# Smaller units for the last input weights, a first expert gathered already transposed, and two residual products moved into the last expert steps

## The reference

```
h = RMSNorm(x)
q,k,v,xr,yr,gates = split(h @ w_in + b_in)
A = attention(rope(rms(q)), rope(rms(k)), v)            # 8 heads, 2 kv heads
R = (rglru_fwd(conv(xr)) + rglru_bwd(conv(xr))) * gelu(yr)
merged = sig(g_A) * (A @ w_attn_o) + sig(g_R) * (R @ w_lru_o)
x = x + merged @ w_out
x = x + MoE(RMSNorm(x))     # top 4 of 32 experts, each w_gu 1024x2048, w_down 1024x1024
out = RMSNorm(x)
```

## Time and profile before

| | |
|---|---|
| runs of the kernel | 1135.7, 1138.17, 1138.58 us; median 1138.17 |
| span of the profiled execution | 1134.2 us (its own device time is not listed; the three runs read 1.5 to 4.4 us more than this span) |
| PE busy | 96% of the span |
| bytes from HBM | 438.2 MB |
| mean granted clock of TensorE | 0.986 |

### The profile page before, as it was taken

One profiled execution on the slowest core, in us unless ns is written; L12 is line 12 of the kernel. 1 busy time (PEld: TensorE's weight loads), 2 busy tenths in 40 slices (PEclk: granted clock), 3 DMA queues, 4 the chain that ended last, 5 costly groups with the idle time before them and its releaser, 6 DMA issues.

```text
span 1134.2 us, 12887 instructions
## 1 busy us (share of the span) xinstructions
PE 1084.8 (96%) x5407; PEld 503.4 (44%) x5407; DVE 371.1 (33%) x645; ACT 237.2 (21%) x369; POOL 2.6 (0%) x10
## 2 busy tenths in 40 slices
PE   7999999999999999999998989898989899899987
PEld 7999899633333333333333333333333333333332
DVE  6997887522212222122121211111211212121212
ACT  5399961211111111111111110011110101010102
POOL 0000000000000000000000000000000000000000
PEclk9999999899999999999999999999999999999999
DMA  9544277999999999999999999999999999999996
GB/s 353 185 178 149 84 287 300 419 425 399 431 425 428 426 434 432 433 426 435 431 429 436 430 430 436 429 430 436 430 432 433 429 436 430 427 427 429 426 428 247
DMA packets 25637, 439.77 MB, mean 388 GB/s; under 512 B 3425, under 2 KB 4065, under 8 KB 6273
## 3 DMA queue, kind: packets, MB, share of 16 engines
q1 hardware_dynamic: 24976, 438.27, 91.5%
q10 hardware_dynamic: 624, 0.99, 0.2%
HBM read 438.20 MB, written 1.05 MB: 387 GB/s over the span
## 4 chain that ended last, share of the span: by engine, by line
PE 67%; DMA 28%; DVE 2%; SPq 1%; ACT 1%; issue 0%; DVEq 0%
PE ps L1491 26%; DMA slots<-in_w_down_dram 22%; PE ps L1500 13%; PE ps L1172 13%; DMA slots<-in_w_gu_dram 5%; PE ps L1455 5%; PE ps L1436 3%; PE ps L1549 2%; DVE slots_r L725 1%; SPq L403 1%; PE ps L1229 1%; PE ps L1450 1%; PE ps L1414 1%; PE ps L1234 0%; PE ps L1526 0%; PE ps L1274 0%
## 5 line engine op out<-in xcount | busy, mean ns | idle before, releaser
L1500 PE MATMUL ps<-slots,lru 128*64 128x512 f32 x1024 | 239.8, 610 | 17.2 <-DMA slots<-in_w_down_dram 17.2
L1491 PE MATMUL ps<-slots,lru 128*64 128x512 f32 x1024 | 227.7, 594 | 11.7 <-DMA slots<-in_w_gu_dram 11.2
L1491 PE MATMUL ps<-slots,qT 128*64 128x512 f32 x984 | 223.8, 596 | 4.6 <-DMA slots<-in_w_gu_dram 4.6
L1491 PEld LDWEIGHTS ps<-slots,lru 128*64 128x64 f32 x1024 | 74.1, 137 | 160.8 <-issue 139.7
L1491 PEld LDWEIGHTS ps<-slots,qT 128*64 128x64 f32 x984 | 68.9, 137 | 152.2 <-issue 144.8
L1500 PEld LDWEIGHTS ps<-slots,lru 128*64 128x64 f32 x1024 | 68.5, 139 | 142.5 <-issue 123.5
L1100 DVE COPY lru<-ps 128x512 f32<-128x512 f32 x32 | 22.1, 692 | 322.9 <-PE ps L1491 322.9
L1172 PE MATMUL ps<-slots_r 128*128 128x256 f32 (+1 forms) x812 | 107.7, 291 | 0.2 <-DVE slots_r L725 0.2
L1172 PEld LDWEIGHTS ps<-slots_r 128*128 128x128 f32 x812 | 102.2, 191 | 5.4 <-issue 2.5
L653 ACT ACTIVATE lru<-ps 128x512 f32<-128x512 f32 x32 | 19.1, 598 | 395.3 <-PE ps L1491 395.3
L1082 DVE TENSOR_SCALAR lru<-sq,rank_col,small 128x64 f32<-128x64 f32 x64 | 17.2, 312 | 241.8 <-PE ps L1436 241.8
(11 more groups left out here) (200 smaller groups left out, 649.3 us busy)
## 6 DMA issues: line engine op xcount, KB each, us to landing
slots<-in_w_gu_dram SPq DMA_DIRECT2D x40, 4096.0 KB, 29.2
slots<-in_w_gu_dram SPq DMA_DIRECT2D x44, 2048.0 KB, 18.9
slots<-in_w_down_dram SPq DMA_DIRECT2D x20, 4096.0 KB, 28.4
slots<-in_w_down_dram SPq DMA_DIRECT2D x22, 2048.0 KB, 20.8
slots<-in_pre_dram SPq DMA_DIRECT2D x13, 2048.0 KB, 8.2
slots<-in_w_down_dram SPq DMA_DIRECT2D x8, 512.0 KB, 31.0
slots<-in_pre_dram SPq DMA_DIRECT2D x3, 1024.0 KB, 6.9
slots<-in_w_gu_dram SPq DMA_DIRECT2D x3, 1024.0 KB, 17.4
```

The costliest lines, as they stand in the source:

```text
L1491: ins = nc.tensor.matmul(ps[64 * side:64 * side + 64, 4 + b, :], xgT[i % 2][:, k, :], rows[r][:, o:o + BANK], start=(k == 0), stop=(k == K ...
L1500: ins = nc.tensor.matmul(ps[64 * side:64 * side + 64, bank, :], actT[(i - 1) % 2][:, k, :], w[:, r, side * BANK:(side + 1) * BANK], start= ...
```

## The change

1. **Units.** Chunks 0 to 7 stay as they are. The seven later chunks become 14 units of 1 MB. A unit needs one slot alone: it lands in the slot's first half, its high part goes to the slot's second half. Each has its own condition for the load (`UNIT_FREED`) and its own two splits. The first four units (projection columns) are read in pieces of 1 KB for a partition and row.
2. **Expert loads.** Slots 2 and 3 are no longer used by input weights once `group` 23 is done, so expert chunks 0 and 1 are issued there; `late` and half of `pbuf` are loaded once the recurrent branch and attention are done; the other slots follow one at a time with the `mix` steps. SLOT_ORDER changes with it.
3. **Mix.** `mix(0)` no longer stands between `branches(3)` and `branches(4)`; six `mix` steps are followed by `mix_end` over the last two blocks.
4. **First expert.** `first_gather` multiplies each 128x128 block of `x2` (as the stationary operand) with the selection (64 columns), which gives the gathered tokens already transposed; ACT's copy, four transposes and one wait go.
5. **Residual products.** The four products before and in step 0 go. In the last four steps, step i = 0 does banks 0 and 1 and step i = 2 does banks 2 and 3, between `gate_up` 2 and `gate_up` 3. The first scatter opens the banks in their place.

```diff
-        SLOT_ORDER = [2, 3, LOWS, SLOTS - 1, 0, 1, 4, 5]
+        UNIT_SLOT = [4, 5, 0, 1, 4, 5, 0, 1, LOWS, 4, 5, 0, 1, LOWS]
+        UNIT_FREED = [(group_done, 16), (group_done, 16), (group_done, 20), (group_done, 20), (group_done, 26),
+                      (group_done, 28), (group_done, 30), (group_done, 32), (gate_ps, 32), (branch_ps, 2),
+                      (branch_ps, 3), (branch_ps, 4), (branch_ps, 6), (branch_ps, 7)]
+        SLOT_ORDER = [2, 3, 4, 5, 0, 1, LOWS, SLOTS - 1]
+        FREED = {2: (group_done, 24), 4: (branch_ps, KD), 5: (mixed_ps, 1), 0: (mixed_ps, 2), 1: (mixed_ps, 3),
+                 LOWS: (mixed_ps, 4)}
...
+            for u in range(4):
+                unit_load(u)
+            for k in range(2):
+                expert_load(k)
+            for u in range(4, 7):
+                unit_load(u)
+            sp.wait_ge(rec_ok, 2)
+            sp.wait_ge(pv_ps, NQ // 2)
             n, j = step_of(EXTRA[0])
             sp.dma_start(late[:, :], expert_src(n, j)).then_inc(extra_full[0], 16)
+            half_load(extra_rows(1, 0), EXTRA[1], 0, extra_full[1])
+            unit_load(7)
+            unit_load(8)
+            half_load(wide[:, 0:2048], 7, 0, slot_full[SLOTS - 1])
+            for u in range(9, 14):
+                unit_load(u)
...
+            def unit_split_high(u):
+                act.wait_ge(*unit_landed(u))
+                nc.scalar.activation(unit_high(u), unit_whole(u), ACT.Copy).then_inc(split_hi, 1)
...
-            gathered_copy(0)
...
-                if g == 1:
-                    split_low(12)
-                if g == 3:
-                    split_low(13)
-                if g == KD - 1:
-                    split_low_by_halves(14)
+                if g != 3:
+                    unit_split_low(7 + g if g < 3 else 6 + g)
...
-            for g in range(4):
+            for g in range(KD):
                 branches(g)
-            mix(0)
-            for g in range(4, KD):
-                branches(g)
-            for c in range(1, 4):
+            for c in range(ENDS):
                 mix(c)
...
+            def first_gather(t):
+
+                for k in range(KD):
+                    ins = nc.tensor.matmul(ps[:, 7, k * CAP:(k + 1) * CAP], x2[:, t, k * P:(k + 1) * P], sel_next[:, t, :],
+                                           start=(t == 0 and k == 0), stop=(t == T - 1 and k == KD - 1))
+                return ins
...
                 gate_up(n, i, 2, single)
                 if i % 2 == 1:
-                    scatter(1 - i // 2, 2)
-                    scatter(1 - i // 2, 3)
+                    scatter(1 - i // 2, 2, opens)
+                    scatter(1 - i // 2, 3, opens)
+                elif single:
+                    residual_in_bank(i)
+                    residual_in_bank(i + 1)
                 gate_up(n, i, 3, single)
```

More of the change, by code:

```diff
@@ L280, in high, with unit_src, unit_whole, unit_low @@
         def high(c):
-            return (late_r if PLACE[c] == LOWS else ring_r[PLACE[c] + 1])[:, 0:WIDTH[c]]
+            return ring_r[PLACE[c] + 1][:, 0:WIDTH[c]]
+        def unit_src(u):
+            c, h = UNITS[u]
+            if u < BR_UNIT:
+                return pre[c].rearrange("p (k n) -> p k n", k=KD)[:, :, h * TOK:(h + 1) * TOK]
+            return pre[c, :, h * UNIT:(h + 1) * UNIT]
+        def unit_whole(u):
+            return ring[UNIT_SLOT[u]][:, 0:UNIT]
+        def unit_low(u):
+            return ring_r[UNIT_SLOT[u]][:, 0:UNIT]
+        def unit_high(u):
+            return ring_r[UNIT_SLOT[u]][:, UNIT:]
+        def unit_landed(u):
+            s = UNIT_SLOT[u]
+            return slot_full[s], 16 * (PLACE.count(s) + UNIT_SLOT[:u + 1].count(s))
+        def unit_high_ok(u):
+            return split_hi, casts_before(CHUNKS) + sum(v not in UNIT_CAST_V for v in range(u + 1))
+        def unit_low_ok(u):
+            return split_lo, CHUNKS + u + 1
         def whole(c):
@@ L735, in split_low, with unit_split_high, unit_split_low @@
                 low_part(low(c), whole(c), high(c)).then_inc(split_lo, 1)
[L737 to L743 removed]
+            def unit_split_high(u):
+                dve.wait_ge(*unit_landed(u))
+                link(high_part(unit_high(u), unit_whole(u)))
+            def unit_split_low(u):
+                if u not in UNIT_CAST_V:
+                    dve.wait_ge(*unit_high_ok(u))
+                low_part(unit_low(u), unit_whole(u), unit_high(u)).then_inc(split_lo, 1)
             lam = cst[:, C_LAM:C_LAM + 16]
@@ L1177, in chunk, with unit @@
                 return [b.rearrange("p (k n) -> p k n", k=k) for b in (high(c), low(c))]
+            def unit(u, k):
+                return [b.rearrange("p (k n) -> p k n", k=k) for b in (unit_high(u), unit_low(u))]
             def transposes(rows, tp0):
@@ L1314, in _ @@
                     values(VALUES_AT.index(i))
-            BLOCKS = CH // P
-            w_br = [chunk(c, BLOCKS) for c in BR_CHUNK]
+            BLOCKS = UNIT // P
+            w_br = [unit(u, BLOCKS) for u in range(BR_UNIT, MIX_UNIT)]
             def branches(g):
                 first = 12 * g
-                for i, c in enumerate(BR_CHUNK[:2]):
-                    if g > 0 and first <= BLOCKS * i < first + 12:
-                        chunk_in(c)
                 if g >= 2:
@@ L1536, in step @@
                     gathered_transposes(n + 1)
-                if first:
-                    residual_in_bank(2)
-                else:
+                if not first:
                     at_least(act_ok, n)
@@ L1550, in step @@
                 ins.then_inc(tp_ps, 1)
-                if first:
-                    residual_in_bank(3)
-                else:
+                if not first:
                     down(n, i, s, 0, range(1, 4))
```

168 lines of the change are left out of this document (79 added, 89 removed).

## The result

The changed kernel takes 1141.16 us (median of 16 runs, 1138.93 to 1144.92) against 1137.55 us for the kernel before beside it: a ratio of 1.0036, 95% interval [1.0028, 1.0043] (the two medians alone give 1.0032). It is 0.36% slower. I had forecast 1136.9 and given "slower" a chance of 0.11.

A forecast was written before the change was run, and what follows sets the result against it. It took PE's progress up to the load issued at 272.18 us (the anchor), not the bytes loaded before, as the bound. The terms summed to -1.25 us, from 1138.17 to 1136.9 us; range 1133.0 to 1140.8.

The forecast's parts named there:

- branch stage: Branch blocks with input units: PE waits 1.6 us ahead of block 3; +1.2 us, between -0.5 and +2.5.
- first gather: Second tile's selection to first expert product: transposed gather shortens it; -1.0 us, between -2.5 and -0.1.
- router: Second tile's router products: a residual product no longer stands ahead of them; -0.15 us, between -0.3 and 0.
- clock, first expert chunk: First expert chunk: runs at half speed in part if the clock returns later; +0.5 us, between 0 and +1.7.
- rest of step 0: End of step 0: transposes no longer held back by a residual product; -1.4 us, between -1.6 and -1.0.
- backlog at the anchor: Load issued at 272.18 us: its landing time of 8.0 against 7.3 isolated; -0.5 us, between -0.7 and 0.
- tail: Last steps: four residual products, 6.9 us, fall into 6.6 us of PE waits; +0.1 us, between 0 and +0.4.
- What bounds the kernel: Up to 272 us: PE's progress, not the bytes loaded before, sets the end; chain through PE alone until 531 us.
- dear end: First gather at the low clock: 0.20 us a weight load, 3.2 us a tile, giving -0.1 us.
- cheap end: First gather at the router products' price, 1.87 us for 16 weight loads, giving -2.5 us.
- R2: Last steps: residual products do not fit into PE's waits; 1140.3 us, or 1143.7 if all four are paid; chance 0.12.
- R3: Gather, clock and branch stage cancel the gains; +2 us, 1140.2; chance 0.13.

The follow-up runs named there:

- experiment 9: Changed kernel with the 4 MB of expert weights for late, pbuf and the wide slot's first half issued behind unit 13: 1136.31 us, 0.9999 of the kernel before.
- experiment 10: Changed kernel with the 4 MB of expert weights behind unit 13, first gather and residual products as before: 1136.39 us, 0.9998 of the kernel before.
- experiment 1: Changed kernel with units 7 and 8 issued ahead of the 3 MB of expert weights for late and pbuf: 1143.55 us, 1.0065 of the kernel before.
- experiment 2: Changed kernel with the first gather as before (two wide products, ACT's copy, four transposes): 1138.41 us, 1.0016 of the kernel before.
- experiment 5: Kernel before with the transposed first gather alone: 1140.45 us, 1.0021 of the kernel before.
- experiment 6: Kernel before with the four residual products moved into the last four steps alone: 1136.11 us, 0.9995 of the kernel before.
- experiment 11: Changed kernel with the 4 MB of expert weights behind unit 13 and the first gather as before: 1136.12 us, 0.9993 of the kernel before.
- experiment 12: Changed kernel, 4 MB of expert weights behind unit 13, first gather as before, two idle products at the first gather: 1135.34 us, 0.9989 of the kernel before.
- experiment 13: Changed kernel, wide gather as before, two idle products there, the 4 MB of expert weights issued between units 11 and 13: 1133.57 us, 0.9973 of the kernel before.
- experiment 16: As experiment 13, with a third idle product behind the transposes that end step 0: 1133.54 us, 0.9972 of the kernel before.
- experiment 3: Changed kernel with the four residual products at their old places between the router and the end of step 0: 1141.68 us, 1.0046 of the kernel before.
- experiment 4: Changed kernel with both the first gather and the residual products as before: 1140.56 us, 1.0034 of the kernel before.
- experiment 7: Changed kernel with units 7 and 8 early, first gather and residual products as before: 1145.22 us, 1.0068 of the kernel before.
- experiment 8: Changed kernel with units 7 and 8 early and the first gather as before: 1147.28 us, 1.0085 of the kernel before.

## Why the prediction was wrong

Two steps failed. The branch stage was priced with a wait of PE but without the low clock that followed it, and the first gather was priced below what its own low-clock row said. A third, a second low spell at step 1, had no term at all. My sum, term by term, as the two profiled executions have it (they are 6.8 us apart, the medians 3.6):

| term | forecast | measured | from |
|---|---|---|---|
| branch stage, to the router products | +1.2 | +3.4 | 211.57 to 214.99 |
| router | -0.15 | -0.3 | 6.20 to 5.87, up to the first gather |
| first gather, both tiles | -1.0 | +0.6 | 8.44 to 9.07, up to the first expert product |
| clock, first expert chunk | +0.5 | +2.1 | 3.65 to 5.78 |
| rest of step 0 | -1.4 | -1.4 | 16.91 to 15.50 |
| clock, first chunk of step 1 | none | +1.7 | 3.65 to 5.35 |
| backlog at the anchor | -0.5 | +0.4 | 8.0 to 8.4 |
| tail | +0.1 | +0.3 | what is left of 6.8 |

- **What bounds the kernel:** right. PE up to the anchor set the end of the changed kernel, and the extra bytes loaded early gave nothing. But the chain did not run through PE alone up to 531 us, as I wrote: from 154.57 to 162.89 it ran over ACT and DVE (the two lines shown above), at the very place where the change then put a later load ahead of DVE's merge.
- **Branch stage: the place was right, the size wrong.** I had the queue, the unit, the merge and the block. PE waited 2.7 in place of 1.6, and block 3 began 1.8 us later than before in place of 1.2. The step that failed is what came next: I priced a block after a wait like one without. Its first 16 products took 3.5, not 2.1, and block 4 came 5.9 us behind block 3 in place of 4.3, which adds the other 1.6 of the 3.4. Experiments 9 and 10 show that this stage loses nothing when no expert weights stand ahead of a unit, and by the ratios (1.0036 against 0.9999) this order of the loads is worth all of the loss. My +1.2 also took unit 7 for the only one at risk; experiment 1 shows that unit 9, issued 9 us later, had less slack than it.
- **First gather: mis-sized, and the sign with it.** I worked the dear end with 0.20 us a record from the warm-up; it was 0.23. The warm-up was no row of the lower level either: the profile gives a granted clock of 1.00 there, while the records get faster from 11 to 20 in 2 us, so 0.20 is a mean over that rise. The windows of the kernel before:

```profile
6.00:8.00 2.00, 2.00 (x11) 2.00 (x10) 0.93 (x7) 1.36 (x3) 0.00 (x0) 1.00 1.04 438
10.00:12.00 2.00, 2.00 (x20) 1.91 (x17) 0.51 (x1) 1.43 (x2) 0.00 (x0) 1.00 1.12 476
```

  Worse, I put the cheap end and my own value on the assumption that the new form might run at the router's price while the old one stayed at 1.98. That 1.98 was itself a low-clock figure; at one level the new form costs twice the old. From the second tile's selection to the first expert product it did fall, from 5.22 to 4.46; the second tile's rank products, which stand behind the first tile's gather and came 1.4 later for it, took that and more. I should have taken the end that I myself had worked out from the clock row. Experiments 2 and 5 put the gather at 0.20% and 0.21%.
- **Clock: mis-sized.** I gave one chunk 0 to 1.7. The spell grew from 6.8 to 13.7 us and cost 2.1 there, and a further one at step 1 cost 1.7, more than the 1.4 that step 0 had gained. I had named this as a sign of being wrong, but put no price on it. Whether the last one is in every run is not known. Five of the 16 runs, the profiled one among them, have a mean clock of 0.980 or 0.981 and a median of 1142.9, the other eleven 0.983 to 0.990 and 1140.4. But a spell of 3.4 us moves the mean clock by 0.0015 only, and the seven short spells behind 550 us count in it just as much, so the mean does not say which spell parts the two groups.
- **Step 0 and the last steps:** right. R2 is false, the products are hidden; experiment 6 confirms both (step 1 begins 1.8 us earlier, and the time does not rise).
- **Backlog:** taken with the wrong sign, and small here. But what I had written off as a cap of 0.7 us is what decides the next step: a kernel whose PE is ahead by more than that gains little unless the bytes come sooner too. Experiments 6, 11, 12 run into it and 13 steps over it.
- **The rivals:** R3, that gather, clock and branch stage cancel the gains, is nearest, but I had called its +2 the bad end of my own terms, and that sum was wrong: the bad ends of the terms, with router and backlog at 0, add up to 2.5 - 0.1 + 1.7 - 1.0 + 0.4 = +3.5, or 1141.7, and the run lies within them. So the upper end of my range was about 1 us too low by my own figures. I had let the three vary apart, though the low clock runs through all of them.

The kernel of experiment 13 or 16 beats both: the units, the wide gather, the residual products in the last steps, the loads for `late` and `pbuf` in the gaps between units 11 and 13, and idle products at the first gather, 0.27 to 0.28% below the kernel before.

## What to carry to other kernels

A load that is moved to an earlier place has a price for what is behind it in the queue; follow each of those to its consumer, since putting the first of them in front hands the wait to the next (2.7 us became 5.7). Put it where the DMA engines are seen standing still, and after that look for the bound again in landing times and not in issues. When a short operation is replaced by another, compare both at the same granted clock, and price a wait of PE with the work that follows it at the lower level.

## What was not expected of the hardware

- A wait of 2.5 to 2.9 us of PE in the midst of full work (changed kernel, experiments 2 to 4) was followed by 16 products in 3.4 to 3.6 us in place of 2.1, in each of four executions, and one of 5.7 to 6.0 us (experiments 1, 7, 8) by 3.4 to 3.8; a wait of 0.56 in the kernel before, by 2.14. How long the low clock lasts is not settled by the wait: 3.4 us behind 5.71, 6.8 us behind 5.97 and 5.94.
- A weight load of 128x128 with 64 columns behind it: 0.125 us a record at the full level, 0.23 at the lower.
- A 1 MB load with nothing ahead of it landed 5.1 us after its issue (the one between 172 and 176 us of the changed kernel, below). The Trainium skill (*DMA: Bandwidth & Descriptors*, section Bandwidth) has 6.15 us for 1 MB, of a transfer issued from GpSimd and counted while its DMA engines are busy; this one, issued from SP and counted from issue to landing, is shorter. In the queue the halved chunks ran at full rate, as forecast.

```profile
slots<-in_pre_dram SPq DMA_DIRECT2D x1, 1024.0 KB, 5.1
```
